# Order of VectorE's work around the first up units and before the last down block of a two-layer trunk

## The chip, the cores and the metric

The kernel runs on one core of one Trainium2 chip. The metric is the time of one execution on the device in microseconds (us); the kernel before was run three times, and its median is the time to compare with.

## The reference

One step of a trunk with two layers over 1,024 prompt tokens and 8 requests of 8 tokens (1,088 columns in all, model width 1,024). Layer 0 is a gated recurrent block, layer 1 a sliding-window attention; each is followed by the same feed-forward block, which is what the change touches:

```python
def conv_ffn(xn, buf, w_up, conv_w, conv_b, w_down):
    u = xn @ w_up
    g, v = u[..., :D_FF], u[..., D_FF:]
    gc, new_buf = causal_dwconv(g, buf, conv_w, conv_b)
    return (jax.nn.gelu(gc) * v) @ w_down, new_buf.astype(buf.dtype)
```

`causal_dwconv` is a depthwise convolution over three positions (three taps), D_FF is 3,072, and all data are float32.

## The kernel before, in words

**Precision.** Every float32 operand of a matmul is split in a high part, which ScalarE copies in a rounded type, and a low part, which VectorE gets by one subtraction. TensorE then does three matmuls for each product (high by high, high by low, low by high). So each weight tile costs ScalarE one instruction (`weight_hi`, `combo_hi`, `prep` on ScalarE) and VectorE one (`weight_lo`, `combo_lo`, `prep` on VectorE), and TensorE waits for the second.

**The up stage.** The 3,072 hidden channels are done in 24 units of 128. A unit computes its gate half and its value half together as a 2x2 block product in seven block products instead of eight (Winograd's form), j = 0 to 6. Their weight tiles live in four slots (a, b, c, a, b, c, d for j = 0 to 6); their token operands are the pieces B11, T1, B21, B22, T2, T3, T4, made from the halves of `x` and split once per layer, during the entry. `product` on TensorE is 24 matmuls of 272 columns. Products 2 and 3 accumulate onto the banks of products 0 and 1, so they must wait until ScalarE has copied those banks out (`product_copy(u, 0)` and `product_copy(u, 1)`, semaphore `p_copied`). Once the banks are summed, GpSimd scales a part (`scale_c12`), ScalarE multiplies the newest tap (`newest_tap`), VectorE adds the two other taps in place (`unit_conv`, four instructions in `y`, tap 1 and then tap 0), ScalarE applies the gelu (`gelu`), and VectorE scales and multiplies (`scale_gelu`, `make_hidden`).

**The entry.** For the first unit of a layer the token pieces are not there yet: `entry` on VectorE has `combo_lo` of the pieces and `weight_lo` of the unit's weights in one order written out by hand. "three" and "two" are the pieces of the first three row pairs or two of them in one instruction; piece 3 is the last. In `first_unit` a product waits at its first matmul for its weights and for the earlier pieces, and at its tenth matmul for piece 3. `entry` also has the weights 0, 1, 2 of unit 1 and the convolution of unit 0; `ffn` goes on with unit 1.

**Engines run in order.** Each engine has one instruction stream, so what stands behind a waiting instruction waits too. ScalarE's stream for unit u is, by its lines in `ffn`:

```python
product_copy(layer, u, 0)
weight_hi(layer, u, 3)
gelu(layer, u - 1)
...
product_copy(layer, u, 1)
```

and `gelu` of unit u - 1 waits for both instructions of tap 0:

```python
act.wait_ge(conv_done, 2 * (KD + gu) + 2)
```

**The down stage.** Of the 24 tiles of hidden rows, 18 are done as three blocks (SB = 3) of six in the same seven-product form, 28 steps each (seven products by four pairs of output tiles p). The last six are the plain block: for each of the eight output tiles a unit of three column pieces (384, 384 and 320 columns). VectorE's loop runs q over the 84 steps: `down_take` of step q - 1 adds TensorE's banks onto their target, `down_weight_lo` splits the weights of step q + 3. In the last nine steps, t = q - 75, it also splits the hidden rows (`hidden_lo`, t = 0 to 5) and the first two weight tiles of the plain block (`prep(n0, 0)` and `prep(n0, 1)`, L2593). The last product takes are L3022, one for each p, in the order p = 0 to 3. TensorE's first plain unit waits for the takes of p = 0, 1, 2, for `prep(n0, 0)` and for the hidden rows; its second unit for the take of p = 3 and `prep(n0, 1)`. ScalarE's parts of both preps come from its own loop. GpSimd adds the pair sums onto `x` after the takes (`finish`, L3654).

Of the kernel before, what the change touches and what calls it, by code (L numbers as in the profile page):

```python
# [20 lines left out]
P = 128  # L21
# [31 lines left out]
FB = 6  # L53
# [52 lines left out]
def build(nc, A):  # L106
    with ExitStack() as ctx:
# [2468 lines left out]
        def _(dve):  # L2576
# [331 lines left out]
            def combo_lo(layer, name, i):  # L2908
                dve.wait_ge(c_hi, combo_at(layer, name, i))
                dve.tensor_tensor(combo_part(layer, name, i, 1), combo_source(name, i), combo_part(layer, name, i, 0).bitcast(F32),  # L2910
                                  ALU.subtract).then_inc(c_lo, 1)
# [123 lines left out]
            def entry(layer, n_first, bias_col=None):  # L3035

                v = (1, 3)[layer]
                for i in range(KD // 2):
                    n = n_first + i
                    for s in range(2):  # L3040
                        last = (i, s) == (KD // 2 - 1, 1)
                        for c in range(2 if last else 3):
                            added(n, i, s, c, bias_col)
                        if s == 1:
                            combo_lo(layer, "T1", i)
                        if last:
                            added(n, i, s, 2, bias_col)
                            break
                        if layer == 0 and i == 0 and s == 0:
                            dve.wait_ge(half_hi, 1)  # L3050
                            dve.tensor_tensor(wlo[0][:, 0:HALF], raw[0][:, 0:HALF], whi[0][:, 0:HALF].bitcast(F32),
                                              ALU.subtract).then_inc(half_lo, 1)
                            dve.wait_ge(hi_ready[0], n + 2)
                            dve.tensor_tensor(wlo[0][:, HALF:], raw[0][:, HALF:], whi[0][:, HALF:].bitcast(F32),
                                              ALU.subtract).then_inc(lo_ready[0], 1)
                        elif i < KD // 2 - 1:
                            prep(n + 1, s, KD * P)
                        else:
                            weight_lo(layer, 0, 0)
                            weight_lo(layer, 0, 1)  # L3060
                        combo_lo(layer, ("B11", "B21")[s], i)

                weight_lo(layer, 0, 2)
                combo_lo(layer, "B22", "three")
                token_inverses(layer)
                combo_lo(layer, "B21", 3)
                weight_lo(layer, 0, 3)
                combo_lo(layer, "B22", 3)
                combo_lo(layer, "T2", "three")
                combo_lo(layer, "T2", 3)  # L3070
                weight_lo(layer, 0, 4)
                combo_lo(layer, "T4", 2)
                combo_lo(layer, "T3", 2)
                combo_lo(layer, "T3", "two")
                combo_lo(layer, "T3", 3)
                weight_lo(layer, 0, 5)
                combo_lo(layer, "T4", "two")
                combo_lo(layer, "T4", 3)
                make_u2(layer, 0)
                weight_lo(layer, 0, 6)  # L3080
                dve.wait_ge(stat_sqrt, roots_base(v) + 3)
                take_c11(layer, 0)
                make_c12(layer, 0)
                weight_lo(layer, 1, 0)
                make_u3(layer, 0)
                weight_lo(layer, 1, 1)
                weight_lo(layer, 1, 2)
                unit_conv(layer, 0)

            entry(0, N_OUT)  # L3090

# [5 lines left out]
            def ffn(layer, n0):  # L3097
                for u in range(1, FT):
                    last = u == FT - 1
                    if u > 1:  # L3100
                        weight_lo(layer, u, 2)
                    make_c21(layer, u - 1)
                    weight_lo(layer, u, 6)
                    weight_lo(layer, u, 3)
                    scale_gelu(layer, u - 1)
                    if last:
                        down_combo_lo(layer, 0, "B11")
                    take_c11(layer, u)
                    weight_lo(layer, u, 4)
                    make_hidden(layer, u - 1)  # L3110
                    weight_lo(layer, u, 5)
                    if last:
                        down_weight_lo(layer, 0, 0, 0)
                    else:
                        weight_lo(layer, u + 1, 0)
                    make_u2(layer, u)
                    make_c12(layer, u)
                    make_u3(layer, u)
                    if last:
                        down_weight_lo(layer, 0, 0, 1)  # L3120
                    else:
                        weight_lo(layer, u + 1, 1)

                    if last:
                        make_c21(layer, FT - 1)
                        unit_conv(layer, u, (1,))
                        down_weight_lo(layer, 0, 0, 2)
                        down_weight_lo(layer, 0, 0, 3)
                        down_combo_lo(layer, 0, "B21")
                        unit_conv(layer, u, (0,))  # L3130
                    else:
                        unit_conv(layer, u)

                for q in range(SB * NQ):
                    b = q // NQ
                    if q > 0 and not copied_out((q - 1) // NQ, (q - 1) % NQ // 4):
                        down_take(layer, (q - 1) // NQ, (q - 1) % NQ // 4, (q - 1) % 4)
                    if 0 < q < SB * NQ - 3:
                        down_weight_lo(layer, (q + 3) // NQ, (q + 3) % NQ // 4, (q + 3) % 4)
                    if q == 3:  # L3140
                        scale_gelu(layer, FT - 1)
                    elif q == 4:
                        make_hidden(layer, FT - 1)
                    early_ones = {5: (0, "T1"), 7: (0, "B22"), 12: (0, "T2"), 15: (0, "T3"), 19: (0, "T4"),
                                  21: (1, "B11"), 26: (1, "B21"), 28: (1, "T1")}
                    if q <= NQ:
                        if q in early_ones:
                            down_combo_lo(layer, *early_ones[q])
                        if q in (9, 17):
                            down_combo_make(layer, 0, "T2" if q == 9 else "T4")  # L3150
                    elif q < SB * NQ - 9:
                        t, g = q % NQ, (q - 1) // 4 + 3
                        if t in (2, 6) and b > 0:
                            down_combo_make(layer, b, "T2" if t == 2 else "T4")
                        if q % 4 == 1 and g < SB * NP:
                            down_combo_lo(layer, g // NP, DOWN[g % NP])
                    else:
                        t = q - (SB * NQ - 9)
                        if t < FB:
                            hidden_lo(layer, t)  # L3160
                        elif t > FB:
                            if t == FB + 1:
                                dve.wait_ge(w_lo, steps_done(layer, SB - 1, NP - 1, 3))
                            prep(n0, t - FB - 1, FB * P)
                down_take(layer, SB - 1, NP - 1, 3)

                if layer == 1:
                    for i in range(KD // 2):
                        for s in range(2):
                            dve.wait_ge(finished, 16 + min(8 + 4 * i, 16))  # L3170
                            for c in range(3):
                                added(n0 + i, i, s, c, None)
                                for kind, job in way_out(i, s, c):
                                    if kind == "y" and job % 2 == 1:
                                        end_copy(job)
                            if i < KD // 2 - 1:
                                prep(n0 + i + 1, s, FB * P)
                    return
                with dve.Fori(0, KD // 2 - 1) as i:
                    dve.wait_ge(finished, 4 * i + 8)  # L3180
                    residual(n0 + i, i, FB * P, low=(1, C_KVN, sb))
                last_residual(n0 + KD // 2 - 1, 2, 1, C_KVN, split_b, KD * P)
# [649 lines left out]
```

## Time and profile before

| what | value |
|---|---|
| median of 3 runs | 2322.27 us (2317.41 to 2323.07) |
| profiled execution, its own time | 2318.29 us |
| its span, first to last instruction | 2316.2 us |
| TensorE busy in the span | 2291.7 us (99%) |
| VectorE, ScalarE, GpSimd busy | 1644.7, 1013.0, 1105.8 us (71%, 44%, 48%) |
| granted TensorE clock, mean | 0.998 of full |

The profile is one execution; all durations in the sections below come from it. The median of the three unprofiled runs lies 4.0 us above its time. Busy time of TensorE counts matmuls that overlap each other, so what matters is where the start of a matmul comes later than the spacing of its kind.

### The profile page before, as it was taken

To read this page: it belongs to the slowest core of one execution; us is meant where nothing else is said; L and a number is where in the kernel's file an instruction comes from. 1 tells how busy PE (TensorE), PEld (TensorE's weight loads), DVE (VectorE), ACT (ScalarE), POOL (GpSimd) and SP (SyncE) were. 2 spreads that over 40 slices of the span, in tenths; PEclk is the share of its full clock that TensorE was granted. 3 is DMA by queue.
4 is the path that set the end of the run, shared out by engine and by line. 5 is a ranking of instruction groups with operands and counts; after the bars stand their busy time and mean duration, and the time that the engine had idled before them with its cause. 6 is when DMAs were issued, how large, how long until landed. Compare 5 with 4: busy or idle time off the path is not lost.

```text
span 2316.2 us, 43244 instructions
## 1 busy us (share of the span) xinstructions
PE 2291.7 (99%) x16916; PEld 2233.9 (96%) x16916; DVE 1644.7 (71%) x2172; ACT 1013.0 (44%) x1732; POOL 1105.8 (48%) x922
## 2 busy tenths in 40 slices
PE   9999999999999999999999999999999999999999
PEld 8999999999999999999999867999999999999999
DVE  7666647777777779986467576467777777789962
ACT  6555645333333334433354585453333333344331
POOL 3222466555555555656220163655555555566540
PEclk9999999999999999999999999999999999999999
DMA  4111132222222324322363102312222223253132
GB/s 136 46 46 46 50 101 84 70 70 83 83 70 69 112 95 170 125 77 85 121 96 93 59 27 97 108 61 84 83 84 64 76 83 92 80 188 136 62 103 91
DMA packets 228790, 203.04 MB, mean 88 GB/s; under 512 B 28373, under 2 KB 209821, under 8 KB 228412
## 3 DMA queue, kind: packets, MB, share of 16 engines
q1 hardware_dynamic: 224180, 188.87, 26.4%
q10 hardware_dynamic: 4404, 12.28, 2.2%
q8 instruction: 82, 1.34, 0.3%
q14 instruction: 60, 0.49, 0.1%
q0 software_dynamic: 64, 0.05, 0.0%
HBM read 152.41 MB, written 50.66 MB: 88 GB/s over the span
## 4 chain that ended last, share of the span: by engine, by line
PE 86%; DVE 6%; issue 3%; DMA 2%; ACT 2%; POOL 1%; SPq 0%; ACTq 0%; DVEq 0%; POOLq 0%
PE ps L1461 14%; PE ps L1460 14%; PE ps L1462 14%; PE ps L1218 10%; PE ps L1220 9%; PE ps L1219 9%; PE ps L1480 3%; PE ps L1481 3%; PE ps L1482 3%; DMA down_raw<-in_f_w_down 1%; PE ps L1701 1%; PE ps L1753 1%; PE ps L1729 1%; DVE ring L2991 1%; DVE later_slots L2985 1%
## 5 line engine op out<-in xcount | busy, mean ns | idle before, releaser
L1480 PE MATMUL ps<-ring,later_slots 128*128 128x272 f32 x960 | 278.2, 290 | 3.5 <-DVE ring L2991 1.8
L1481 PE MATMUL ps<-ring,later_slots 128*128 128x272 f32 x960 | 276.6, 288 | 0.0
L1482 PE MATMUL ps<-ring,later_slots 128*128 128x272 f32 x960 | 274.8, 286 | 0.0
L2963 DVE SCALAR_TENSOR_TENSOR y<-convin,fcol,y 128x1024 f32<-128x1024 f32 x192 | 225.9, 1216 | 16.3 <-ACT y L2181 14.7
L1460 PE MATMUL ps<-b,slot_a 128*128 128x272 f32 x768 | 221.5, 288 | 2.1 <-DVE slot_a L2917 2.1
L1461 PE MATMUL ps<-b,slot_a 128*128 128x272 f32 x768 | 221.3, 288 | 0.0
L1462 PE MATMUL ps<-b,slot_a 128*128 128x272 f32 x768 | 220.5, 287 | 0.0
L1480 PEld LDWEIGHTS ps<-ring,later_slots 128*128 128x128 f32 x960 | 180.8, 188 | 6.0 <-DVE later_slots L2985 3.7
L1482 PEld LDWEIGHTS ps<-ring,later_slots 128*128 128x128 f32 x960 | 181.6, 189 | 0.0
L1481 PEld LDWEIGHTS ps<-ring,later_slots 128*128 128x128 f32 x960 | 181.5, 189 | 0.0
L1218 PE MATMUL ps<-sa,whi 128*128 128x384 f32 (+1 forms) x540 | 177.3, 328 | 1.4 <-DVE x L3022 1.3
L1220 PE MATMUL ps<-sa,wlo 128*128 128x384 f32 (+1 forms) x540 | 176.2, 326 | 0.0
L1219 PE MATMUL ps<-sa,whi 128*128 128x384 f32 (+1 forms) x540 | 176.1, 326 | 0.0
L1218 PE MATMUL ps<-sb,whi 128*128 128x384 f32 (+1 forms) x468 | 158.6, 339 | 1.3 <-DVE x L3022 1.3
L3558 POOL TENSOR_TENSOR wsum<-rawu 128x512 f32<-128x512 f32 x48 | 63.3, 1319 | 195.9 <-DVE slot_c L2917 178.7
L1220 PE MATMUL ps<-sb,wlo 128*128 128x384 f32 (+1 forms) x468 | 152.7, 326 | 0.0
L1219 PE MATMUL ps<-sb,whi 128*128 128x384 f32 (+1 forms) x468 | 152.6, 326 | 0.0
L1460 PEld LDWEIGHTS ps<-b,slot_a 128*128 128x128 f32 x768 | 144.7, 188 | 2.9 <-DVE slot_a L2917 2.8
L1462 PEld LDWEIGHTS ps<-b,slot_a 128*128 128x128 f32 x768 | 144.5, 188 | 0.0
L1461 PEld LDWEIGHTS ps<-b,slot_a 128*128 128x128 f32 x768 | 144.5, 188 | 0.0
L3570 POOL TENSOR_TENSOR wsum<-rawu 128x512 f32<-128x512 f32 x48 | 109.2, 2276 | 63.8 <-DVE slot_a L2917 63.8
L2593 DVE TENSOR_TENSOR wlo<-raw,whi 128x1024 fp32r<-128x1024 f32 (+1 forms) x59 | 79.1, 1340 | 78.9 <-ACT whi L1863 78.8
(503 smaller groups left out, 7878.2 us busy)
## 6 DMA issues: line engine op xcount, KB each, us to landing
rawu<-in_f_w_up SPq DMA_DIRECT2D x192, 256.0 KB, 4.3
h_spill<-x SPq DMA_DIRECT2D x48, 544.0 KB, 3.1
down_raw<-in_f_w_down SPq DMA_DIRECT2D x48, 384.0 KB, 4.2
part<-h_spill SPq DMA_DIRECT2D x30, 544.0 KB, 5.2
f_spill<-x ACTq DMA_DIRECT2D x16, 544.0 KB, 2.7
x<-f_spill SPq DMA_DIRECT2D x16, 544.0 KB, 8.6
raw<-in_a_w_in SPq DMA_DIRECT2D x16, 512.0 KB, 4.0
last_rows<-h_spill SPq DMA_DIRECT2D x12, 544.0 KB, 5.2
```

What stands on the lines that cost most here:

```text
L1218: pe.matmul(out, whi[s][:, w], mhi[k][:, chunk(c)], start=(k == 0), stop=False)
L1219: pe.matmul(out, whi[s][:, w], mlo[k][:, chunk(c)], start=False, stop=False)
L1220: last = pe.matmul(out, wlo[s][:, w], mhi[k][:, chunk(c)], start=False, stop=(k == nk - 1))
L1460: pe.matmul(out, hi[:, i, :], b_hi, start=(i == 0 and not more), stop=False, skip_group_check=more)
L1461: pe.matmul(out, hi[:, i, :], b_lo, start=False, stop=False, skip_group_check=more)
L1462: last = pe.matmul(out, lo[:, i, :], b_hi, start=False, stop=(i == 3), skip_group_check=more)
L1480: pe.matmul(out, slot[:, 0, i, :], b_hi, start=(i == 0 and not more), stop=False, skip_group_check=more)
L1481: pe.matmul(out, slot[:, 0, i, :], b_lo, start=False, stop=False, skip_group_check=more)
L1482: last = pe.matmul(out, slot[:, 1, i, :], b_hi, start=False, stop=(i == 2), skip_group_check=more)
L2593: dve.tensor_tensor(wlo[s][:, 0:cols], raw[s][:, 0:cols], whi[s][:, 0:cols].bitcast(F32), ALU.subtract)\
L2963: ins = dve.scalar_tensor_tensor(out, g, fcol[:, u, col + t:col + t + 1], out, ALU.mult, ALU.add)
L3570: ins = pool.tensor_tensor(wsum[:, 0, :, :], a11, a21, ALU.subtract)
```

## The change

Three edits, all in VectorE's stream. In the entry, the low splits of the first unit's weights 4 and 5 come ahead of the last token piece of T2 and of T3. The convolution of unit 0 is cut in its tap 1 and its tap 0, and the low splits of unit 1's weights 6 and 3, which stood behind `make_c21(0)` in `ffn`, come between them. In the down loop both preps of the plain block come one step sooner: at t = 6 and 7 instead of 7 and 8. The numbers of instructions and the streams of all other engines stay as they are. The entry and the loop run once in each of the two layers.

```diff
                 combo_lo(layer, "T2", "three")
+                weight_lo(layer, 0, 4)
                 combo_lo(layer, "T2", 3)
-                weight_lo(layer, 0, 4)
                 combo_lo(layer, "T4", 2)
                 combo_lo(layer, "T3", 2)
                 combo_lo(layer, "T3", "two")
+                weight_lo(layer, 0, 5)
                 combo_lo(layer, "T3", 3)
-                weight_lo(layer, 0, 5)
...
                 weight_lo(layer, 1, 2)
-                unit_conv(layer, 0)
+                unit_conv(layer, 0, (1,))
+                weight_lo(layer, 1, 6)
+                weight_lo(layer, 1, 3)
+                unit_conv(layer, 0, (0,))
...
                     make_c21(layer, u - 1)
-                    weight_lo(layer, u, 6)
-                    weight_lo(layer, u, 3)
+                    if u > 1:
+                        weight_lo(layer, u, 6)
+                        weight_lo(layer, u, 3)
                     scale_gelu(layer, u - 1)
...
                         if t < FB:
                             hidden_lo(layer, t)
-                        elif t > FB:
-                            if t == FB + 1:
+                        elif t < FB + 2:
+                            if t == FB:
                                 dve.wait_ge(w_lo, steps_done(layer, SB - 1, NP - 1, 3))
-                            prep(n0, t - FB - 1, FB * P)
+                            prep(n0, t - FB, FB * P)
```

## Rows read from the trace of the kernel before

**Rows 1.** The page: busy us (share of the span), instructions of each engine.

```profile
PE 2291.7 (99%) x16916; PEld 2233.9 (96%) x16916; DVE 1644.7 (71%) x2172; ACT 1013.0 (44%) x1732; POOL 1105.8 (48%) x922
```

**Rows 2.** Waits of TensorE, whole span: us in total, times, longest us.

```profile
PE ps L1218 <- DVE x L3022: 2.6, 2, 1.3
...
PE ps L1460 <- DVE slot_a L2917: 2.1, 3, 1.4
```

**Rows 3.** TensorE's timeline, first unit of layer 0: start, duration, line, idle before.

```profile
374.44 0.36 PE L1460 MATMUL ps<-t2c,slot_b 128*128 128x272 f32 x1 [0.86 <-DVE slot_b L2917]
...
377.95 0.40 PE L1460 MATMUL ps<-t3c,slot_c 128*128 128x272 f32 x1 [0.25 <-DVE slot_c L2917]
...
381.07 0.33 PE L1460 MATMUL ps<-t4c,slot_d 128*128 128x272 f32 x1
```

**Rows 4.** VectorE's timeline, first unit of layer 0.

```profile
373.50 0.68 DVE L2917 TENSOR_TENSOR slot_b<-wsum,slot_b 128x512 fp32r<-128x512 f32 x1
...
380.29 0.67 DVE L2917 TENSOR_TENSOR slot_d<-rawu,slot_d 128x512 fp32r<-128x512 f32 x1
```

**Rows 5.** TensorE's timeline at product 3 of unit 1, layers 0 and 1.

```profile
393.04 0.29 PE L1462 MATMUL ps<-b,slot_c 128*128 128x272 f32 x1
393.80 0.39 PE L1460 MATMUL ps<-b,slot_a 128*128 128x272 f32 x1 [0.48 <-DVE slot_a L2917]
...
1557.05 0.29 PE L1462 MATMUL ps<-b,slot_c 128*128 128x272 f32 x1
1558.70 0.39 PE L1460 MATMUL ps<-b,slot_a 128*128 128x272 f32 x1 [1.36 <-DVE slot_a L2917]
```

**Rows 6.** VectorE's timeline from the convolution of unit 0, layer 0.

```profile
388.05 3.86 DVE L2963 SCALAR_TENSOR_TENSOR y<-convin,fcol,y 128x1024 f32<-128x1024 f32 x4 [1.70 <-ACT y L2181]
...
393.06 0.68 DVE L2917 TENSOR_TENSOR slot_a<-wsum,slot_a 128x512 fp32r<-128x512 f32 x1
```

**Rows 7.** ScalarE's timeline there: weight 3, gelu, copy; the copy of layer 1.

```profile
389.15 0.63 ACT L2157 ACTIVATE slot_a<-wsum 128x512 fp32r<-128x512 f32 x1
...
391.94 1.21 ACT L2172 ACTIVATE y<-y,fcol 128x1088 f32<-128x1088 f32 x1 [0.86 <-DVE y L2963]
393.06 0.60 ACT L2166 ACTIVATE t<-ps 128x544 f32<-128x544 f32 x1
...
1557.95 0.60 ACT L2166 ACTIVATE t<-ps 128x544 f32<-128x544 f32 x1
```

**Rows 8.** VectorE's timeline, end of layer 0's down stage, and one later split.

```profile
1062.13 1.34 DVE L3022 SCALAR_TENSOR_TENSOR x<-ps,x 128x544 f32<-128x544 f32 x2
1063.40 1.77 DVE L2593 TENSOR_TENSOR wlo<-raw,whi 128x768 fp32r<-128x768 f32 x1
1065.09 0.71 DVE L3022 SCALAR_TENSOR_TENSOR x<-ps,x 128x544 f32<-128x544 f32 x1
1065.72 1.45 DVE L2593 TENSOR_TENSOR wlo<-raw,whi 128x768 fp32r<-128x768 f32 x1
...
1087.25 0.96 DVE L2593 TENSOR_TENSOR wlo<-raw,whi 128x768 fp32r<-128x768 f32 x1 [2.59 <-ACT whi L1863]
```

**Rows 9.** GpSimd's timeline there, and one add while VectorE idles.

```profile
1062.99 3.37 POOL L3654 TENSOR_TENSOR x<-x,t 128x544 f32<-128x544 f32 x2 [4.70 <-DVE x L3022]
...
1070.33 1.36 POOL L3649 TENSOR_TENSOR x<-x,sum_rest 128x544 f32<-128x544 f32 x1
```

**Rows 10.** TensorE's timeline at the start of the plain block, layers 0 and 1.

```profile
1064.43 0.28 PE L1482 MATMUL ps<-ring,later_slots 128*128 128x272 f32 x1
1066.01 0.41 PE L1218 MATMUL ps<-sa,whi 128*128 128x384 f32 x1 [1.30 <-DVE x L3022]
...
2230.44 0.41 PE L1218 MATMUL ps<-sb,whi 128*128 128x384 f32 x1 [1.29 <-DVE x L3022]
```

**Rows 11.** Stretches: length; busy and count of PE, PEld, DVE, ACT, POOL; clock; DMA, GB/s.

```profile
1527.00:1530.00 3.00, 3.00 (x15) 3.00 (x15) 1.07 (x3) 2.62 (x5) 3.00 (x3) 0.50 0.00 0
...
1064.00:1067.00 3.00, 1.70 (x12) 1.52 (x11) 3.00 (x3) 0.00 (x0) 2.94 (x4) 1.00 0.14 41
```

## The prediction, made before the changed kernel was run

> **What bounds the kernel now.** First the busy times on the page: TensorE works in 99% of the span [rows 1], so only what makes a matmul start later or earlier than the one before it allows can change the time. Then TensorE's own waits over the whole span: they add up to a few us, and two of the longer entries are places that the change touches, the wait for VectorE's take L3022 (two times, 1.3 us at most, once a layer) and for the low split of slot a (three times, 1.4 us at most) [rows 2]. So at the very best a few us are to be had, where 0.3%, about what a measurement of this kernel can tell from no change, is 7 us. Then the timelines of the four engines around these places, read in parallel: what finished just before each late matmul, and what would have finished next had that come earlier.
>
> **Edit 1, the first unit's weights 4 and 5.** Product 4 starts at 374.44 behind VectorE's split of weight 4, which starts at 373.50 and takes 0.68, so it ends at 374.18; product 5 waits for its own split at 377.95 [rows 3, 4]. One place sooner, each split passes one token piece of the same kind of work (0.6 to 0.7 for 544 columns where nothing slows it), so product 4 can start about 0.8 us and product 5 about 0.65 us sooner. The piece that is passed is needed only at the tenth matmul of the product, some 1.2 us in, and is done by then. But what is late next is weight 6: VectorE has no idle entry ahead of its split from 373.50 on, the order change leaves the amount of work ahead of it alone, and it ends at 380.29 + 0.67 = 380.96, while product 6 starts at 381.07 [rows 3, 4]. The gain is given back there within one product: at most 0.11 us stays, and a restart after a wait costs about 0.1 us (the first matmul after one takes 0.36 to 0.40 where 0.28 to 0.29 is usual). I put this edit at 0 in both layers. Its bounds are -0.1 and +0.1 a layer.
>
> **Edit 2, weights 6 and 3 of unit 1 between the two taps.** Product 3 of unit 1 starts at 393.80, where the last matmul of product 2 started at 393.04 and the usual spacing is 0.13: 0.63 us are lost. In layer 1 it is 1558.70 against 1557.05, so 1.52 lost [rows 5]. The wait is put down to slot a's low split: it starts at 393.06 and takes 0.68, so it ends at 393.74 [rows 5, 6]. The edit does take that away: the split of weight 3 can run as soon as tap 1 is done, since ScalarE's high part starts at 389.15 and takes 0.63 [rows 7]. But product 3 has a second condition, the copy of product 1's banks, and that copy stands behind the gelu of unit 0 in ScalarE's stream. The gelu starts at 391.94, right at the end of the convolution (388.05 + 3.86 = 391.91), the copy starts at 393.06 and ends at 393.66 [rows 6, 7]. So the copy was only 0.08 us ahead of the split that the trace names. With two splits between the taps, the end of the convolution moves back by them. GpSimd reads nothing during them, as it then waits for the convolution, so each goes at the undisturbed rate: from 393.06 back, make_c21 and the two splits follow each other at about 0.60 each, which makes 1.20. Convolution 391.91 to 393.11, gelu and copy follow in the same distances, the copy ends at 394.86, and product 3 starts about 0.07 later at 394.93: 1.13 us later than before. In layer 1 the copy ended at 1557.95 + 0.60 = 1558.55, becomes 1559.75, and product 3 starts at 1559.82, 1.12 later than 1558.70 [rows 5, 7]. The bounds a layer: +1.1 as worked out, or -0.63 and -1.52 if the copy should not hold product 3 (then it follows product 2 directly). I take +1.13 and +1.12, since both ends of the chain are in the rows. Nothing gives it back later: the entry's first half cannot, because the convolution's start hangs on the loaded weights of unit 1 and GpSimd's scaling, which the edit leaves alone, and in the following units TensorE has no wait to shrink [rows 2]. Behind the later convolution stand make_c21, scale_gelu, take_c11 and the split of weight 4 of unit 1, needed one product (3 us) later, so they are covered.
>
> **Edit 3, the plain block's preps one step sooner.** Before, VectorE's order is take p = 0 and p = 1 (1062.13, two in 1.34), prep 0 (1063.40, 1.77), take p = 2 (1065.09, 0.71), prep 1 (1065.72, 1.45), take p = 3. TensorE has issued its last step at 1064.43 and starts the plain block at 1066.01, 0.20 after the take of p = 2 ends [rows 8, 10]. VectorE runs here without a gap, behind TensorE, so the order alone decides. The new order is take 0, prep 0, take 1, prep 1, take 2, take 3: prep 1, which TensorE wants only some 9 us later (its second unit), now stands ahead of the take that TensorE waits for. What this costs is the length of prep 1, less what prep 0 may gain. A prep of this size is 0.96 us alone, and 1.77 and 1.45 beside GpSimd's two adds from 1062.99 to 1066.36, where one such add alone is 1.36 [rows 8, 9]. Now prep 0 is issued at 1062.13 + 0.64 = 1062.77, before GpSimd's first add at 1062.99, so I take it as undisturbed: the next instruction starts 0.89 later, take 1 at 1063.66, prep 1 at 1064.30. GpSimd's add comes behind prep 0 and ends at about 1065.1; prep 1 ends 0.81 after an add that it waits for (before: 1067.17 against 1066.36), so at 1065.9. Take 2 then ends at 1066.54 and the plain block starts at 1066.74: 0.73 us later. Bounds: prep 1 alone at 0.9 with prep 0 sped up by 0.8 gives +0.1; prep 1 at 1.7 with prep 0 as slow as before gives +1.7; with both as before it is +1.4. I take +0.73 in each layer. In layer 1 the plain block starts at 2230.44 after the same wait of 1.29 [rows 10].
>
> The same two preps bear on a rule of the Trainium skill (SBUF — State Buffer, Who interferes with whom): a VectorE instruction with both inputs in SBUF and a GpSimd instruction that reads SBUF block each other, and the one that issues first goes first. The stretched preps of this trace agree with that; by the rule edit 3 would cost about 0.7 a layer, and with the durations simply carried over 1.4.
>
> **Sum.** 1.13 + 1.12 + 2 x 0.73 + 0 = +3.7 us. The profiled execution's own time is 2318.29, so it would be 2322.0; the median of the three runs is 4.0 above that execution, and 2322.27 + 3.7 = 2326.0 is the forecast: 0.16% slower, not to be told from no change.
>
> **The rivals.**
>
> *Slower by more than 0.3%: the wider holes cost clock.* The granted clock is not always full. In the stretch 1527 to 1530 it was 0.50, which is 1.2 of 2.4 GHz, and TensorE issued 15 matmuls in 3 us where the usual spacing of 0.13 gives 24 [rows 11]: that is 1.1 us lost in these 3 us, and since the slow stretch goes a little past them at both ends, I put one such drop at 1.7. Ahead of it TensorE had done its token sums, matmuls of two columns. Against this rival: the hole at 1064 to 1066 left the clock at 1.00 [rows 11]. For it: the change widens these holes, from 1.6 to 2.3 us at the plain block, from 0.76 to 1.9 and from 1.65 to 2.8 at product 3, and makes them wider than the one that passed at full clock. Each drop adds 1.7; two of the four places make 3.7 + 3.4 = 7.1, which is the point from which it decides, and all four make 10.5. Time: 2329.4 to 2332.8. Chance 0.21.
>
> The Trainium skill (TensorE: Matmul & The Clock Gate, Part 1) says that the array falls to half clock after it has been idle and comes back after sustained work. The 0.50 stretch agrees in the level; the rule would count for this rival, and its chance above is from how wide the holes get.
>
> *A little faster: the split, not the copy, held product 3.* The trace names the split of slot a in both layers [rows 5]. If the copy's condition is met earlier than I read it, product 3 follows product 2 directly: -0.63 - 1.52 = -2.15, plus edit 3 at +1.46 makes -0.7, so 2321.6; with edit 3 at its low bound 2320.3. Against it stand the order of ScalarE's stream and the copy's end at 393.66 [rows 7]. Chance 0.12.
>
> *Edit 3 does what it says and is free or better.* The preps are hidden if TensorE does not reach the takes in time anyway. Against it: the take of p = 2 ends 0.20 before the plain block starts in a hole of 1.6 us [rows 8, 10]. Time 2322.27 + 2.25 = 2324.5; it lies in the forecast's own range, and I give it 0.05.
>
> *Faster by more than 0.3%.* It would need 7 us, more than the waits named in [rows 2] hold; only a clock drop less in each layer and the rival above together come near (-0.7 - 3.4 = -4.1). Chance 0.04 with whatever else I do not see.
>
> **How the numbers follow.** The forecast has 0.58 and its own range from the bounds: 2.25 + 0.2 = +2.5 to 2.25 + 3.4 + 0.2 = +5.9, so 2324.8 to 2328.2. The median of the three runs itself may sit elsewhere in 2317.4 to 2323.1, and single drops of the clock (+1.7) blur the upper end. With the little-faster rival at the low end (2320) and the first half of the clock rival at the upper (2331), the range 2320 to 2331 leaves out 2 in 10. Within 0.3%: 0.58 + 0.12 + 0.05 = 0.75; slower 0.21; faster 0.04.
>
> **What would show it.** In the changed profile: products 4 and 5 of the first unit start earlier, product 6 at the same distance from the entry; product 3 of unit 1 starts right behind ScalarE's copy, about 6.9 us after the convolution's start instead of 5.75, and its wait is put down to ScalarE, not to slot a's split. At the plain block both preps stand ahead of the last two takes, and the hole before L1218 is about 2.3 us instead of 1.6. Wrong would be: product 3 directly behind product 2 (then the copy never held it), a hole at the plain block no wider than before (then VectorE was not the one behind), or stretches at clock 0.50 after these holes.

## The result, and the profile after

Over 15 runs each, the changed kernel takes 2324.96 us (median; 2322.07 to 2328.55), the kernel before 2319.92 (2317.41 to 2323.07). The ratio on record is 1.0019, 95% interval [1.0012, 1.0027]: 4.4 us more, between 2.8 and 6.3 (the two medians lie 5.0 us apart). That is inside the 0.3% that the prediction called not to be told from no change, though with 15 runs the sign is clear. The profiled execution took 2324.88 us.

The page, span and busy times, to be held against [rows 1]:

```profile
span 2322.9 us, 43248 instructions
...
PE 2293.8 (99%) x16916; PEld 2236.7 (96%) x16916; DVE 1642.5 (71%) x2172; ACT 1013.6 (44%) x1732; POOL 1106.3 (48%) x922
```

The span grew by 6.7 us and TensorE's busy time by 2.1, with the same 16916 matmuls. So in 4.6 of the 6.7 us TensorE has nothing in flight; in the rest it is busy longer with the same matmuls. TensorE's waits over the whole span (us in total, times, longest) say where, against [rows 2]:

```profile
PE ps L1460 <- ACT t L2166: 4.6, 2, 2.6
PE ps L1218 <- DVE x L3022: 3.7, 2, 1.9
...
PE ps L1460 <- DVE slot_d L2917: 0.8, 2, 0.4
...
PE ps L1460 <- DVE slot_a L2917: 0.2, 1, 0.2
```

The wait for slot a's split has shrunk from 2.1 to 0.2 us, as the change meant. In its place stands a wait that was not in the list: ScalarE's copy L2166, 4.6 us in two places. The take L3022 went from 2.6 to 3.7, and weight 6 of the first unit (slot d) is new with 0.8.

**Edit 1.** TensorE's timeline in the first unit of layer 0 (start, duration, line, idle before), against [rows 3]:

```profile
373.94 0.36 PE L1460 MATMUL ps<-t2c,slot_b 128*128 128x272 f32 x1 [0.20 <-DVE slot_b L2917]
...
377.45 0.39 PE L1460 MATMUL ps<-t3c,slot_c 128*128 128x272 f32 x1 [0.26 <-DVE slot_c L2917]
...
381.15 0.39 PE L1460 MATMUL ps<-t4c,slot_d 128*128 128x272 f32 x1 [0.42 <-DVE slot_d L2917]
```

Products 4 and 5 start 0.50 us sooner, and product 6 has a wait that it did not have: 381.15 against 381.07. The whole entry is 0.16 us later in this execution (the first matmul of product 1, on T1 and slot b, starts at 363.19 here and at 363.03 before), so product 6 is 0.08 sooner at its place, and nothing more is left.

**Edit 2.** The three timelines around product 3 of unit 1 in layer 0: TensorE, VectorE, ScalarE.

```profile
393.16 0.29 PE L1462 MATMUL ps<-b,slot_c 128*128 128x272 f32 x1
395.51 0.36 PE L1460 MATMUL ps<-b,slot_a 128*128 128x272 f32 x1 [2.06 <-ACT t L2166]
```

```profile
388.56 2.34 DVE L2963 SCALAR_TENSOR_TENSOR y<-convin,fcol,y 128x1024 f32<-128x1024 f32 x2 [1.70 <-ACT y L2181]
390.93 0.69 DVE L2917 TENSOR_TENSOR slot_d<-rawu,slot_d 128x512 fp32r<-128x512 f32 x1
391.54 0.68 DVE L2917 TENSOR_TENSOR slot_a<-wsum,slot_a 128x512 fp32r<-128x512 f32 x1
392.14 1.48 DVE L2963 SCALAR_TENSOR_TENSOR y<-convin,fcol,y 128x1024 f32<-128x1024 f32 x2
```

```profile
393.65 1.20 ACT L2172 ACTIVATE y<-y,fcol 128x1088 f32<-128x1088 f32 x1 [2.07 <-DVE y L2963]
394.76 0.60 ACT L2166 ACTIVATE t<-ps 128x544 f32<-128x544 f32 x1
```

Slot a's split ends at 392.22, before product 2 has issued its last matmul, and TensorE still stands until 395.51. Read it backwards: the copy ends at 395.36, it follows the gelu, and the gelu follows tap 0, which the two splits moved back. From the convolution's start to product 3 it is 6.95 us, where it was 5.75 [rows 5, 6]. From the last matmul of product 2 to product 3 it is 2.35 us, where it was 0.76, and in layer 1 2.84, where it was 1.65. In layer 0 that is 1.59 more and not 1.20, because the convolution itself starts 0.51 us later (388.56 against 388.05) and product 2 only 0.12.

**Edit 3.** The end of layer 0's down stage on VectorE, GpSimd and TensorE (its last line from layer 1), against [rows 8 to 10]:

```profile
1064.38 0.71 DVE L3022 SCALAR_TENSOR_TENSOR x<-ps,x 128x544 f32<-128x544 f32 x1
1065.01 0.94 DVE L2593 TENSOR_TENSOR wlo<-raw,whi 128x768 fp32r<-128x768 f32 x1
1065.88 0.71 DVE L3022 SCALAR_TENSOR_TENSOR x<-ps,x 128x544 f32<-128x544 f32 x1
1066.51 1.47 DVE L2593 TENSOR_TENSOR wlo<-raw,whi 128x768 fp32r<-128x768 f32 x1
1067.91 1.34 DVE L3022 SCALAR_TENSOR_TENSOR x<-ps,x 128x544 f32<-128x544 f32 x2
```

```profile
1065.23 3.94 POOL L3658 TENSOR_TENSOR x<-x,t 128x544 f32<-128x544 f32 x2 [4.70 <-DVE x L3022]
```

```profile
1066.69 0.28 PE L1482 MATMUL ps<-ring,later_slots 128*128 128x272 f32 x1
1068.83 0.41 PE L1218 MATMUL ps<-sa,whi 128*128 128x384 f32 x1 [1.86 <-DVE x L3022]
...
2235.51 0.52 PE L1218 MATMUL ps<-sb,whi 128*128 128x384 f32 x1 [1.88 <-DVE x L3022]
```

Prep 0 is issued 0.22 us ahead of GpSimd's first add and takes 0.94 instead of 1.77; prep 1 waits behind the add and takes 1.47; the take of p = 2 comes after both. The hole is 2.14 us, start to start, where it was 1.58. In layer 1 the first matmul after it lasts 0.52 instead of 0.41: the clock had fallen.

Stretches behind the holes (length; busy and count of PE, PEld, DVE, ACT, POOL; granted clock; DMA share, GB/s), to be held against [rows 11]:

```profile
396.00:399.00 3.00, 3.00 (x16) 3.00 (x15) 3.00 (x4) 0.41 (x1) 0.00 (x0) 0.50 0.00 0
...
1066.00:1069.00 3.00, 1.14 (x9) 0.95 (x8) 3.00 (x4) 0.00 (x0) 3.00 (x2) 1.00 0.49 131
2236.00:2239.00 3.00, 3.00 (x11) 3.00 (x10) 0.00 (x0) 0.00 (x0) 2.92 (x3) 0.50 0.39 118
```

The same two stretches at 396 and 2236 in the profile of before:

```profile
396.00:399.00 3.00, 3.00 (x26) 3.00 (x25) 3.00 (x4) 1.26 (x2) 0.51 (x2) 1.00 0.14 46
...
2236.00:2239.00 3.00, 3.00 (x24) 2.79 (x23) 0.56 (x1) 1.07 (x2) 3.00 (x3) 1.00 0.00 0
```

At two of the four places, behind product 3 in layer 0 and behind the hole at the plain block in layer 1, TensorE runs at 0.50 of its clock (1.2 of 2.4 GHz). Neither stretch was slow in the profile of before. Away from the four places both profiles have slow stretches too: both have one near 1381, the one before has the one at 1527 [rows 11] and one at 11 to 15, and this one has one from 1434 to 1437.

**Where the 6.7 us of the profile went.** Both traces have the same 16916 matmuls in the same order, so each can be held against itself. The four holes put them back by 1.6, 0.6, 1.2 and 0.6 us, 3.9 together. The two slow stretches behind the holes add 1.5 and 1.6, 3.1 together. The slow stretch at 1434 adds 1.5. That the one at 1527 is not there gives back only 0.2: without it the matmuls run faster, but then they wait for VectorE in the first unit of layer 1. The remaining 1.6 us are gained far from the edits, mainly near 950, 2040 and 2115, where the profile of before has small delays that this one has not. So in these two executions the holes and the clock behind them come to 7.0 us.

### The profile page after: what moved, and what is told of

It reads as the page before. It is cut to its first block, busy times and chain, and to the rows that moved or that the text cites. A ratio compares the mean times of both kernels' runs of the same rounds, so it can differ in the third digit from the quotient of the medians.

```text
span 2322.9 us, 43248 instructions
## 1 busy us (share of the span) xinstructions
PE 2293.8 (99%) x16916; PEld 2236.7 (96%) x16916; DVE 1642.5 (71%) x2172; ACT 1013.6 (44%) x1732; POOL 1106.3 (48%) x922
## 4 chain that ended last, share of the span: by engine, by line
PE 90%; DVE 4%; issue 3%; ACT 2%; POOL 1%; DMA 1%; SPq 0%; ACTq 0%; DVEq 0%; POOLq 0%
PE ps L1461 14%; PE ps L1462 14%; PE ps L1460 14%; PE ps L1218 9%; PE ps L1220 9%; PE ps L1219 9%; PE ps L1480 5%; PE ps L1481 5%; PE ps L1482 4%; PE ps L1701 1%; PE ps L1729 1%; PE ps L1753 1%; DVE y L2963 1%; PE ps L1624 0%; PE ps L1617 0%
```

## The experiments

Each experiment ran 11 or 12 times beside 21 to 35 runs of the kernel before on the same chip. The table has the sum of what TensorE's timeline shows at the places that the edit touches (gaps from the start of one matmul to the start of the next, against the profile of before), the ratio, and the mean of the granted clock over all runs. The first unit of layer 1 is left out of the sums, because the profile of before has its slow stretch there. The clock is recorded in steps of 0.001 a run, and 0.001 of this kernel's time is 2.3 us. For the kernel before the mean clock was 0.9962 beside the first four experiments, 0.9965 beside the next three and 0.9964 beside the last two, each group on a chip of its own; for its runs beside the changed kernel the clock of only one is on record.

| kernel | gaps at its places, us | ratio, 95% interval | mean clock |
|---|---|---|---|
| changed kernel | +3.9 | 1.0019 [1.0012, 1.0027] | 0.9958 |
| edit 1 alone | about 0 | 1.0004 [0.9995, 1.0012] | 0.9963 |
| edit 2 alone | +2.8 | 1.0012 [1.0004, 1.0021] | 0.9967 |
| edit 3 alone | +1.2 | 1.0017 [1.0008, 1.0025] | 0.9955 |
| changed, copy ahead of gelu | +3.0 | 1.0015 [1.0006, 1.0023] | 0.9958 |
| before, copy ahead of gelu | +0.1 | 1.0008 [0.9999, 1.0017] | 0.9963 |
| before, only prep 0 sooner | -1.6 | 0.9993 [0.9984, 1.0002] | 0.9965 |
| three splits, copy first, prep 0 | -3.4 | 0.9978 [0.9969, 0.9987] | 0.9976 |
| edit 3, hole filled | +1.1 | 1.0003 [0.9994, 1.0012] | 0.9973 |
| before, hole filled | 0 | 0.9999 [0.9990, 1.0008] | 0.9962 |

### Edit 1 alone

```diff
+                weight_lo(layer, 0, 4)
                 combo_lo(layer, "T2", 3)
-                weight_lo(layer, 0, 4)
...
+                weight_lo(layer, 0, 5)
                 combo_lo(layer, "T3", 3)
-                weight_lo(layer, 0, 5)
```

> The kernel before with edit 1 alone: in the entry the low splits of weights 4 and 5 of the first unit stand one token piece earlier. Theory: products 4 and 5 start about 0.8 and 0.65 us sooner, product 6 waits for the split of weight 6 and starts where it did, so the time stays (0 us, ratio 1.0000 within its interval) and unit 1 is as before. Rival: the gain of product 4 is kept, which would be -0.5 to -1 us a layer, a ratio of 0.9993 or less.

1.0004 with no change in its interval. The gap ahead of product 4 is 0.52 us instead of 1.15, and what was won is waited for at product 6, from TensorE's timeline:

```profile
380.70 0.29 PE L1462 MATMUL ps<-t3c,slot_c 128*128 128x272 f32 x1
381.41 0.39 PE L1460 MATMUL ps<-t4c,slot_d 128*128 128x272 f32 x1 [0.42 <-DVE slot_d L2917]
```

0.71 here, 0.12 before: 0.63 won, 0.59 given back. In layer 1 the profile of before can't be compared, for its slow stretch at 1527. But the profile of edit 2 alone, which has neither edit 1 nor that stretch, shows a gap of 0.71 us ahead of product 4 there, and this one shows 0.71 ahead of product 6 instead: the wait only moved.

### Edit 2 alone

```diff
-                unit_conv(layer, 0)
+                unit_conv(layer, 0, (1,))
+                weight_lo(layer, 1, 6)
+                weight_lo(layer, 1, 3)
+                unit_conv(layer, 0, (0,))
...
-                    weight_lo(layer, u, 6)
-                    weight_lo(layer, u, 3)
+                    if u > 1:
+                        weight_lo(layer, u, 6)
+                        weight_lo(layer, u, 3)
```

> The kernel before with edit 2 alone: weights 6 and 3 of unit 1 split between the two taps. Theory: product 3 of unit 1 starts about 6.9 us after the convolution's start instead of 5.75, its wait is put down to ScalarE's copy, +2.2 us in both layers together, with a clock drop behind the hole up to +1.7 more for each: ratio 1.0010 to 1.0022. Rival (the split alone held the product): product 3 directly behind product 2, about -2 us, ratio 0.9991.

1.0012, with the interval clear of 1 and of the rival's 0.9991. TensorE's timeline in layer 0:

```profile
393.06 0.29 PE L1462 MATMUL ps<-b,slot_c 128*128 128x272 f32 x1
395.46 0.36 PE L1460 MATMUL ps<-b,slot_a 128*128 128x272 f32 x1 [2.11 <-ACT t L2166]
```

The convolution starts at 388.51 in this execution, so it is again 6.95 us from there. In the two layers the gaps grew by 1.64 and 1.20. The first is larger than the 1.20 of the chain because the convolution itself started 0.46 later (388.51 against 388.05) with product 2 at the same place: that start hangs on GpSimd, which waits for a transfer to land, and it wanders. In the run with edit 3 alone, whose entry is untouched, the convolution starts at 388.58, and this gap is 1.22 instead of 0.76. Behind the hole this profile has a slow stretch too, from 396.8 to 400.2; its time lies in neither of the two gaps.

### Edit 3 alone

```diff
-                        elif t > FB:
-                            if t == FB + 1:
+                        elif t < FB + 2:
+                            if t == FB:
                                 dve.wait_ge(w_lo, steps_done(layer, SB - 1, NP - 1, 3))
-                            prep(n0, t - FB - 1, FB * P)
+                            prep(n0, t - FB, FB * P)
```

> The kernel before with edit 3 alone: both preps of the plain block one step sooner. Theory: the hole before the plain block goes from 1.58 us to about 2.15 (the second prep stands ahead of the take of p = 2, the first one loses its stretch beside GpSimd), +0.6 us a layer, +1.2 in all, and up to +1.7 more where the clock drops behind it: ratio 1.0005 to 1.0015. Rival (the preps are hidden): hole 1.58, ratio 1.0000.

```profile
1063.91 0.28 PE L1482 MATMUL ps<-ring,later_slots 128*128 128x272 f32 x1
1066.07 0.41 PE L1218 MATMUL ps<-sa,whi 128*128 128x384 f32 x1 [1.87 <-DVE x L3022]
```

The hole is 2.16 us in layer 0 and 2.15 in layer 1, as worked out. The ratio, 1.0017, is more than the 1.2 us of holes explain: 3.9 us (1.9 to 5.8). The profiled execution itself took 2317.95 us with the clock at 0.998, the shortest of its 11 runs; the two runs with the lowest clocks (0.993 and 0.994) took 2325.69 and 2325.10. So the same instructions in the same order take up to 7.7 us more or less, and the clock goes along with it. The profile itself shows no slow stretch behind either of its two holes; the runs that lost clock were not profiled, so where they lost it is not shown. The last pair of kernels takes this up.

### The changed kernel with the copy ahead of the gelu

The kernel is the changed one, and on ScalarE:

```diff
                     weight_hi(layer, u, 3)
+                    if u == 1:
+                        product_copy(layer, u, 1)
                     gelu(layer, u - 1)
                     if last:
                         down_combo_hi(layer, 0, "B11")
-                    product_copy(layer, u, 1)
+                    if u > 1:
+                        product_copy(layer, u, 1)
```

> The changed kernel with one more edit, on ScalarE: for unit 1 the copy of product 1's banks stands ahead of the gelu of unit 0 instead of behind it. If the copy is what holds product 3 in the changed kernel, product 3 now follows product 2 directly (start to start 0.13 us instead of 2.4). But I expect the chain gelu, scale_gelu, take_c11, split of weight 4 to hold product 4 then, about 0.7 us in layer 0 and 1.6 in layer 1, so that no more than the 2.2 us of edit 2 come back: the time lies 2 to 4 us below the changed kernel's, ratio to the kernel before 1.0000 to 1.0010. Rival (something else than the copy holds product 3): product 3 stays 6.9 us behind the convolution's start, ratio 1.0019 as the changed kernel. A second rival: nothing behind it is late, and the time falls by 4.4 us, ratio 0.9998 or less.

The copy does hold product 3: with it moved, product 3 starts at 393.56, 0.13 behind the last matmul of product 2. But the gain is nearly gone one product later. TensorE, VectorE and ScalarE in layer 0:

```profile
396.44 0.29 PE L1462 MATMUL ps<-b,slot_a 128*128 128x272 f32 x1
398.40 0.39 PE L1460 MATMUL ps<-t2c,slot_b 128*128 128x272 f32 x1 [1.67 <-DVE slot_b L2920]
```

```profile
395.27 1.84 DVE L2976 TENSOR_TENSOR y<-y,rstd 128x1088 f32<-128x1088 f32 x1 [0.64 <-ACT y L2172]
397.03 0.71 DVE L2928 TENSOR_TENSOR convin<-ps,rstd 128x544 f32<-128x544 f32 x1
397.67 0.68 DVE L2920 TENSOR_TENSOR slot_b<-wsum,slot_b 128x512 fp32r<-128x512 f32 x1
```

```profile
394.03 1.21 ACT L2172 ACTIVATE y<-y,fcol 128x1088 f32<-128x1088 f32 x1 [1.35 <-DVE y L2966]
```

Weight 4 stands behind scale_gelu and take_c11 on VectorE, and these behind the gelu. Product 4 waits 1.96 us (2.30 in layer 1) where product 3 had waited 2.35 (2.84). So my expectation named the next wait rightly and mis-sized it: 0.7 and 1.6 were worked out from the gelu of the kernel before, which edit 2 had since moved back by 1.2. It said 1.0000 to 1.0010 and came out at 1.0015. The gelu starts 5.10 us after the convolution's start, where it is 5.09 in the changed kernel, so the earlier copy did not delay it. The experiment therefore also shows that the bound of -0.63 and -1.52, "follows product 2 directly", could not have been had: what product 3 wins, product 4 loses.

### The kernel before with the copy ahead of the gelu

The same edit on ScalarE, nothing else.

> The kernel before with the copy of product 1's banks of unit 1 ahead of the gelu on ScalarE, and nothing else. Theory: in the kernel before, slot a's split and the copy ended within 0.08 us of each other; with the copy early the split alone holds product 3, the wait stays (0.76 and 1.65 us start to start), ratio 1.0000. Rival (the copy alone held it): product 3 directly behind product 2, -2.1 us, ratio 0.9991.

```profile
394.70 0.29 PE L1462 MATMUL ps<-b,slot_c 128*128 128x272 f32 x1
395.58 0.39 PE L1460 MATMUL ps<-b,slot_a 128*128 128x272 f32 x1 [0.59 <-DVE slot_a L2920]
```

The wait stays, 0.88 and 1.61 us. So in the kernel before either condition alone was enough to hold product 3, and taking away one of them could win next to nothing.

### Only prep 0 sooner

```diff
-                        elif t > FB:
-                            if t == FB + 1:
+                        elif t in (FB, FB + 2):
+                            if t == FB:
                                 dve.wait_ge(w_lo, steps_done(layer, SB - 1, NP - 1, 3))
-                            prep(n0, t - FB - 1, FB * P)
+                            prep(n0, (t - FB) // 2, FB * P)
```

> The kernel before with only the first of the two preps one step sooner: take 0, prep 0, take 1, take 2, prep 1, take 3. Theory: prep 0 is issued before GpSimd's first add and takes 0.94 instead of 1.77 us, and nothing else is put ahead of the take of p = 2: the hole before the plain block goes from 1.58 to about 0.75 us, -0.8 a layer, -1.6 in all, ratio 0.9993. Rival (order does not matter to the stretch): the hole stays at 1.58, ratio 1.0000.

VectorE and TensorE, end of layer 0's down stage:

```profile
1061.52 0.71 DVE L3022 SCALAR_TENSOR_TENSOR x<-ps,x 128x544 f32<-128x544 f32 x1
1062.15 0.94 DVE L2593 TENSOR_TENSOR wlo<-raw,whi 128x768 fp32r<-128x768 f32 x1
1063.02 1.34 DVE L3022 SCALAR_TENSOR_TENSOR x<-ps,x 128x544 f32<-128x544 f32 x2
```

```profile
1064.57 0.41 PE L1218 MATMUL ps<-sa,whi 128*128 128x384 f32 x1 [0.46 <-DVE x L3022]
```

The hole is 0.75 us, less than half of before. Half of edit 3 is worth -0.8 us a layer, the other half, prep 1 ahead of the take of p = 2, costs 1.4. The ratio, 0.9993, is what the holes give, but its interval still holds 1, so the gain is shown in the trace and not in the time.

### A version that beats both

It has the order of the preps from the previous kernel, and edit 1 is taken back. Ahead of tap 0 it splits weight 4 as well. On ScalarE for unit 1 the copy and the high part of weight 4 stand ahead of the gelu, and VectorE splits weight 5 ahead of `make_hidden`. Against the changed kernel, without the lines of edit 1 and of the preps:

```diff
                 unit_conv(layer, 0, (1,))
                 weight_lo(layer, 1, 6)
                 weight_lo(layer, 1, 3)
+                weight_lo(layer, 1, 4)
                 unit_conv(layer, 0, (0,))
...
                     if u == 1:
                         product_copy(layer, u, 1)
+                        weight_hi(layer, u, 4)
                     gelu(layer, u - 1)
...
-                    weight_lo(layer, u, 4)
-                    make_hidden(layer, u - 1)
+                    if u > 1:
+                        weight_lo(layer, u, 4)
+                        make_hidden(layer, u - 1)
                     weight_lo(layer, u, 5)
+                    if u == 1:
+                        make_hidden(layer, u - 1)
```

> A version meant to beat both: the order of the preps of the previous kernel; weights 6, 3 and 4 of unit 1 split between the two taps; on ScalarE for unit 1 the copy of product 1's banks and the high part of weight 4 ahead of the gelu; on VectorE the split of weight 5 ahead of make_hidden for unit 1. Expected: product 3 directly behind product 2 (0.63 and 1.52 us won), products 4 and 5 within 0.2 us of theirs, the plain block 0.8 us sooner in each layer: -3.4 to -3.7 us, ratio 0.9985. Rival (a later condition, weight 5's high part or GpSimd behind the later convolution, takes the gain): only -1.6 us, ratio 0.9993.

0.9978 [0.9969, 0.9987]: 5.1 us below the kernel before, the only one of all whose interval lies below 1. The gaps at product 3 are gone in both layers, both plain blocks start 0.8 us sooner, and one new gap of 0.56 has appeared (product 6 of unit 1 in layer 1, for make_u2). The stretch where the changed kernel runs 16 matmuls at 0.50 has 26 at 1.00:

```profile
396.00:399.00 3.00, 3.00 (x26) 3.00 (x25) 3.00 (x4) 1.15 (x2) 0.49 (x1) 1.00 0.02 5
```

The gaps add up to -3.4 us, which leaves 1.7. The mean clock is 0.0011 higher than that of the kernel before beside it, which would be some 2.6 us, so the rest fits the clock. The four parts of this version were not run one by one, the preps excepted.

### The hole at the plain block, filled

On TensorE, before the first plain unit's waits, in each layer; once on edit 3 alone, once on the kernel before:

```diff
+                    if s == 0:
+                        event, count = taken_at(layer, SB - 1, NP - 1, 0)
+                        pe.wait_ge(event, count)
+                        for _ in range(8):
+                            pe.matmul(ps[:, 0, 0:HC], later_slots[:, 3, 0, 0, :], down_combo(layer, SB - 1, "T4")[:, 0, 0, 0:HC],
+                                      start=True, stop=True)
```

> Edit 3 alone, with eight matmuls of 272 columns added on TensorE in front of the plain block in each layer; they write a bank that the plain block overwrites and only fill the wait. Edit 3 alone showed +1.2 us of wider holes in its profile, but a ratio of 1.0017 (about 3.9 us), and a mean clock over its 11 runs of 0.9955 against 0.9962 of the kernel before. Theory: what goes past the 1.2 us is clock lost behind the wider hole; filled, the hole has no more idle time than the kernel before has, the mean clock comes back to 0.9962 or more, and the ratio falls to 1.0003 to 1.0010. Rival (the rest has nothing to do with the clock): ratio 1.0017 as without them.

> The kernel before with the same eight matmuls in front of the plain block. They fit in its hole of 1.58 us with 0.6 to spare, so they cost nothing by themselves: ratio 1.0000 to 1.0002 if they keep the clock as it is, up to 0.0005 less if that hole cost clock in the kernel before too. Rival: they delay the first piece, +0.5 us a layer or more, ratio 1.0004.

TensorE in edit 3 with the filling, layer 0:

```profile
1063.38 0.28 PE L1482 MATMUL ps<-ring,later_slots 128*128 128x272 f32 x1
1063.50 1.16 PE L1546 MATMUL ps<-ring,later_slots 128*128 128x272 f32 x8
1065.52 0.41 PE L1218 MATMUL ps<-sa,whi 128*128 128x384 f32 x1 [0.87 <-DVE x L3028]
```

The plain block starts 2.14 us after the last down matmul, as late as in edit 3 alone, but about half of that time is now filled. The ratio is 1.0003 instead of 1.0017, and the mean clock over the runs is 0.9973 instead of 0.9955. On the kernel before, the same matmuls change nothing (0.9999, clock 0.9962). So more work in the same wait went with some 3 us less, which points to the clock for what edit 3 cost beyond its 1.2 us of waiting. The two intervals overlap by a little (1.0008 to 1.0012), and the two kernels ran on different chips (the kernel before took 2319.01 us on the one and 2319.04 on the other). Neither profile has a slow stretch at the plain block. So I call the direction well supported, the size (3 us) rough, and the place where the clock was lost not shown.

## Why the prediction was right

It said 2326.0 us, and +3.7 against the kernel before; measured were 2324.96, and +4.4 by the ratio. That the absolute time fits within 1.0 us is in part luck: the kernel before, 2322.27 over three runs, came down to 2319.92 over 15, which is 2.35 us less to start from, and the two medians then lie 1.3 us further apart than forecast.

**Edit 1 at 0.** Right, by the step it named: product 6 waits for weight 6, behind a VectorE with no idle time. Of the 0.6 us won at product 4 (0.8 was worked out), 0.08 or less stays.

**Edit 2 at +1.13 and +1.12.** Right in its mechanism: the copy behind the gelu, 0.08 us behind which the named split had hidden it. The chain from the convolution's start grew by 1.20 (5.75 to 6.95). The 0.07 more is the start of the matmul, 0.15 after the copy ends instead of the 0.07 that I took. The gap ahead of product 3 grew by 1.19 in layer 1, but by 1.59 in layer 0, because the convolution started later there. The forecast took this start as fixed, which it is not. Two experiments bear the near tie out from both sides: the split alone moved leaves the copy (1.0012), the copy alone moved leaves the split (1.0008, no gain).

**Edit 3 at +0.73 a layer.** Right in its mechanism, a little large: the hole grew by 0.56 and 0.59. The order of events came out as worked out, prep 0 ahead of GpSimd's add at 0.94 and prep 1 behind it; the estimate had prep 1 end 0.17 us too late. So instead of 1.46 the two holes cost 1.15. The rule that I had weighed (the Trainium skill, SBUF — State Buffer, Who interferes with whom: who issues first goes first) agrees with the trace: the prep issued 0.22 us ahead of the add is not stretched, and the pair of adds takes 3.94 where it took 3.37.

**The sum** was 3.7, and the gaps of the changed kernel's profile add up to 3.9. They agree that well because 0.5 us too little in edit 2 and 0.3 too much in edit 3 nearly cancel. That the ratio says 4.4 [2.8 to 6.3] leaves room for half a us of the clock rival as the middle value, and for 2.4 us at most.

**The rival of the clock** got 0.21 as a whole. As the case that decides (more than 0.3%) it did not come. As a mechanism it is there: slow stretches follow two of the four widened holes in the profile, and this is one of the three things that the prediction itself had named as a sign of being wrong. There they cost 3.1 us, close to the 3.4 that the prediction had put at two drops. Between the two kernels less of it shows: the kernel before loses clock as well, at other places, and its profiled execution was 1.6 us faster than its median, while that of the changed kernel sat at its own. The mean clock over the runs is 0.9958 against 0.9962 to 0.9965 of the kernel before, which ran on other chips. An estimate from this difference is 0.9 to 1.6 us. In the changed kernel's runs the six with a clock of 0.997 or more have a median of 2323.4 us, the eight with 0.995 or less one of 2326.7. The prediction left it out of the forecast's sum; an average of half a us to 1.6 us belonged in there, and for edit 3 alone more.

**The rival of the split** (a little faster) fell by the experiment that moves the copy: there product 3 is free, and in the changed kernel it is not. Its price of -2.15 us was wrong too, since the next wait, at product 4, costs 1.83 and 2.18 us, more than product 3 wins.

**Still open:** why edit 2 alone has a mean clock of 0.9967 in spite of its wider holes (the difference to 0.9962 may be noise), and whether the effects of the three edits on the clock add. Measured separately they cost 0.9, 2.8 and 3.9 us, 7.6 together, where the change as a whole costs 4.4. With intervals of about 2 us on each, part of that is noise; whether where a hole comes decides more than how wide it is was not tested.

## What to carry to other kernels

A trace names the last of several conditions. Before you take that one away, work out when the others are met: here the second one came 0.08 us earlier, on another engine, behind work that the change itself moved back. When work is moved ahead in an in-order queue, count everything that it passes: of two preps moved one step sooner, one won 0.8 us and the other lost 1.4, since the consumer waited for the take between them and not for the second prep. On a kernel whose TensorE hardly rests, a hole of 2 us can cost more than its own length: behind two of the four holes here, half clock added 1.5 and 1.6 us. A slow stretch costs less where the matmuls would have waited anyway: the one at 1527 cost 0.2.

## What the runs showed of the hardware

Half clock came behind some of the holes between dense matmuls and not behind others of the same width. The stretch from 395.9 in the changed kernel came behind a hole of 2.35 us, the one in layer 1's plain block behind 2.16; the holes of 2.14 and 2.84 in the same execution left no slow stretch right behind them. In all eleven profiles the feed-forward blocks (first up units and start of the plain block) have eleven holes of 2.1 to 2.9 us, and four of them were followed by half clock within 1.4 us; of the 27 holes from 1.0 to 2.0 us there, none was. These are too few, in too few executions, to make a limit of. In 3 us at half clock TensorE issued 16 matmuls of 272 columns, where the kernel before and the best version issued 26, which is 1.25 us of work at the spacing of 0.125. The Trainium skill (TensorE: Matmul & The Clock Gate, HAM oscillation — how this bites in real kernels) gives as its abstract rule to avoid idle gaps, and the gaps that it means are longer than any of these; the trace does not agree, as the clock fell behind gaps of 2.16 and 2.35 us. The same instructions in the same order took 2317.95 to 2325.69 us from run to run of edit 3 alone. A single profile can thus not price a clock effect over the runs, and 11 runs do so only roughly.
